# Routing of a mixture-of-experts stage: token rows stored without their shift, ranks by pairs, a gather straight from the table, four PSUM banks for the first expert

## The chip, the cores and the metric

One core of a Trainium2 chip runs the whole program. The metric is device time in microseconds (us) of one execution, the median of the runs shown. The engines are TensorE (PE; its weight loads stand apart as PEld), VectorE (DVE), ScalarE (ACT), GpSimd (POOL, which issues the DMAs with indices) and SyncE (SP, which issues the weight loads). Each runs its own instructions in order; they wait for each other by semaphores.

## What is computed

One layer of token mixers over 512 tokens of width 2048, then a grouped top-2 mixture-of-experts feed-forward, then an RMS norm. The change lies between the two: in the routing, and in how an expert's token block is read.

```python
hl2 = rmsnorm(xl, norm2_w[i]) * (1 + mod_l[4]) + mod_l[3]        # mod_l[3] is "m3" in the kernel

def moe_ffn(h, w_router, router_bias, w1, w3, w2):               # T = 512, 16 experts in 4 groups
    scores = sigmoid(h @ w_router)
    sel = scores + router_bias
    grp = sel.reshape(T, 4, 4)
    g_idx = argmax(top_k(grp, 2)[0].sum(-1))                     # best group by its two best experts
    _, loc = top_k(in_grp, 2)                                    # two experts of that group
    gate = gate / sum(gate)
    # tokens are sorted by expert into blocks of 128; a block is one expert's
    yblk = (silu(xblk @ w1[e]) * (xblk @ w3[e])) @ w2[e]
    # the two outputs of a token are weighted by gate and added
```

## The kernel before, in words

All matrices are fp32. A product is made of three matmuls on a high and a low part in fp32r: ACT writes the high part as a cast, DVE subtracts it from the source to give the low part.

**Rows.** DVE builds `x2` (tokens after the mixers) and `h2 = x2 * n2`, both `[128, 4, 2048]`: four tiles of 128 tokens. `normed(t)` (L1797) turns tile t into `h2 * inv_rms + m3` with `m3_row`, a row of 2048 values repeated on all partitions, and POOL stores it to `h2_d` in DRAM (L2160; the profile calls the tensor `h_rows`, and drops digits from all names, so that `m3_row` is `m_row`).

**Routing.** It is one chain on DVE. After the logits (L1802, L1805) ACT takes the sigmoid (L1281). `rank` (L1816 to L1825) gives each of four values its place by comparing with each other one: a memset, and six comparisons each followed by an addition. It runs over 64 values (experts) and again over 16 (groups). From the ranks come `chosen_r`, the gates, and from PE a count (L910, L912); after that `normed(2)` and `normed(3)`, then the places of the tokens, `in_block`, the one-hot `slot_1` (L1886), and from PE (L918) the table `table_i` (L1898): for each block the 128 token numbers. `step` waits for the instruction just issued. PE fills the time with `keep_busy` matmuls (L904), whose results nobody reads.

**Gather.** POOL copies a column of the table to `idx_now` (L2168), waits for the copy, and issues an indirect DMA (L2171) that brings 128 rows of `h2_d` into `xe`. It waits before the first for the table and for the landing of all four row tiles (`y_out`).

**Experts.** For each of 16 experts: `turn_x(b, part)`, part 0 to 3, four PE transposes each (L952) of `xe` into PSUM bank `6 + part % 2`; `x_hi` on ACT (L1292) casts the bank to `xe_hi`; `x_lo` on DVE (L1903) makes `xe_lo` from bank and `xe_hi`. There are two banks, so `turn_x` of a part waits for `x_lo` two parts back (L949; the semaphore `xe_rdy` begins at 2). Then come 24 units of weights, 128x1024 each and 6 matmuls each: 16 for the two up matrices, 8 for the down matrix. SP loads two units per DMA into one of 6 slots `e_raw` (L551), ACT casts (L1288, `e_hi`), DVE subtracts (L1809, `e_lo`).

The first expert stands outside a loop: its four `turn_x`, `x_ready(0)`, 16 up units, then the four `turn_x(1, ...)`. The loop `Fori(1, E)` runs 15 times over 24 units q: 16 up units of expert e, 8 down units of expert e - 1, and after units 17 to 20 a `turn_x` of expert e + 1:

```python
for q in range(24):                       # DVE, L1941 and after; PE and ACT alike
    e_lo_unit(e * 24 + (n - 8), n + 4)    # n = q + 5: five units ahead of PE
    if q == 3: act_lo(e - 1)
    if q == 9: silu(e)
    if q == 17: gate_up(e, ...)
    if 18 <= q <= 21: x_lo(e + 1, q - 18)
```

**Loads around the routing.** SP issues e_raw loads 0 to 3 early; load 4 waits for all four `normed`, load 5 for the landing of the stored rows, load 6 for the gather.

Of the kernel before, what the change touches and what calls it, by code (L numbers as in the profile page):

```python
# [32 lines left out]
P = 128  # L33
# [16 lines left out]
E = 16  # L50
# [80 lines left out]
def build(nc, x, c, ctx_tokens, c_ctx, w_ada, b_ada, norm1_w, norm2_w, w_in, w_pool_group, pool_scale,  # L131
# [22 lines left out]
    with stack:  # L154
# [119 lines left out]
        x2T = Room(nc, base, 90, 98).new("x2T", [P, 4, SEQ], F32)  # L274
        m3_row = Room(nc, base, 154, 162).new("m3_row", [P, D], F32)
        rt_room = Room(nc, base, 194, 198)
# [18 lines left out]
        gate_w = keep.new("gate_w", [P, 2, NTOK], F32)  # L295
        table_i = keep.new("table_i", [P, NBLK + 1], I32)
        idx_now = keep.new("idx_now", [P, 1], I32)
        route_i = keep.new("route_i", [P, 8], I32)
# [6 lines left out]
        block_tok = tb.new("block_tok", [P, 2 * NTOK, NBLK], F32)  # L305
        block_tok_r = tb.new("block_tok_r", [P, 2 * NTOK, NBLK + 1], F32R)
        slot_1 = tb.new("slot_1", [P, 2 * NTOK, P], F32R)

# [45 lines left out]
        def halves(pair, first, width, half):  # L354

            return bass.AP(pair.tensor, first, [[2 * SEQ, P], [2 * half, width // (2 * half)], [SEQ + half, 2],
                                                [1, half]])

        def bank(b, n=512):
            return ps[:, b, 0:n]  # L360
# [96 lines left out]
        def _(sp):  # L457
# [99 lines left out]
            for n in range(8):  # L557
                if n == 2:
                    sp.wait_ge(x2_rdy, 20)
                if n == 3:  # L560
                    sp.wait_ge(part_mm, 4)
                if n == 4:
                    sp.wait_ge(h2_rdy, NTOK)
                if n == 5:
                    sp.wait_ge(y_out, 16 * NTOK)
                if n == 6:
                    sp.wait_ge(xe_in, 16)
                load_e(n, n % EP, piece(0, n))
# [21 lines left out]
        def _(pe):  # L590
# [311 lines left out]
            def keep_busy(n):  # L902
                for _ in range(n):
                    mm(bank(UB), upper_r[:], m_hi[:, 8, :], start=True, stop=True)  # L904

            keep_busy(28)
            pe.wait_ge(sel_rdy, 1)
# [14 lines left out]
            pe.wait_ge(table_rdy, 1)  # L922
            keep_busy(24)

# [19 lines left out]
            def turn_x(b, part):  # L944

                if part == 0:
                    pe.wait_ge(xe_in, b * 16 + 16)

                pe.wait_ge(xe_rdy, b * 4 + (part + 1))  # L949
                pe.wait_ge(actT_rdy, b + 1)  # L950
                for j in range(4):
                    last = pe.transpose(ps[:, 6 + part % 2, j * P:(j + 1) * P],  # L952
                                        xe[:].rearrange("t (p k) -> t k p", k=KT)[:, 4 * part + j, :], ident[:])
                last.then_inc(xe_T, 1)
# [8 lines left out]
            def x_ready(b):  # L963
                pe.wait_ge(xe_rdy, b * 4 + 6)

            for part in range(4):
                turn_x(0, part)
            x_ready(0)
            for q in range(16):
                up_unit(q, q % EH, q % 8, q // 8)  # L970
            for part in range(4):
# [47 lines left out]
        def _(act_e):  # L1019
# [260 lines left out]
            act_e.wait_ge(lg_step, LG_RDY)  # L1280
            activate(rt[:, 0, :], rt[:, 3, :], ACT.Sigmoid).then_inc(lg_step, 1)  # L1281


# [27 lines left out]
            for q in range(AHEAD):  # L1311
                e_hi_unit(q, q, 16 * (q // 2 // EP + 1))
            act_e.wait_ge(table_rdy, 1)
            for part in range(4):
                x_hi(0, part)
# [60 lines left out]
        def _(dve):  # L1376
# [403 lines left out]
            modulated(3, 0)  # L1780
            dve.wait_ge(units_done, 2 + S_W + 32)
            own.did(dve.tensor_copy(ones_r[:], ones[:]))
            own.did(dve.memset(SM(15), 0.0))
# [27 lines left out]

            def rank(value, out, scratch, width):

                v, o, s = (a.rearrange("p (g a) -> p g a", a=4) for a in (value, out, scratch))
                n = width // 4
                step(dve.memset(out, 0.0))  # L1816
                for b in range(4):
                    if b < 3:
                        r = s[:, :, b + 1:4]
                        step(tt(r, v[:, :, b:b + 1].to_broadcast([P, n, 3 - b]), v[:, :, b + 1:4], ALU.is_ge))  # L1820
                        step(tt(o[:, :, b + 1:4], o[:, :, b + 1:4], r, ALU.add))
                    if b > 0:
                        r = s[:, :, 0:b]
                        step(tt(r, v[:, :, b:b + 1].to_broadcast([P, n, b]), v[:, :, 0:b], ALU.is_gt))
                        step(tt(o[:, :, 0:b], o[:, :, 0:b], r, ALU.add))  # L1825

            normed(1)
            dve.wait_ge(lg_step, LG_SCORE)
            step(tt(R3(1), R3(0), bias_row[:].unsqueeze(1).to_broadcast([P, NTOK, E]), ALU.add))
            rank(R(1), R(2), R(3), NTOK * E)  # L1830
# [3 lines left out]
            rank(SM(0), SM(1), SM(2), NTOK * GROUPS)  # L1834
            win_g = SM(3)
# [13 lines left out]

            normed(2)  # L1850
            normed(3)
            dve.wait_ge(pos_mm, 1)
# [141 lines left out]
        def _(pool):  # L1994
# [140 lines left out]
            pool.dma_start(bias_row[:], router_bias.partition_broadcast(P)).then_inc(rows_in, 16)  # L2135
            pool.dma_start(m3_row[:], mod_d[0, D:2 * D].partition_broadcast(P)).then_inc(rows_in, 16)

# [131 lines left out]
```

## Time and profile before

| what | value |
|---|---|
| median of 3 runs (lowest, highest) | 2394.51 us (2394.19, 2394.67) |
| the profiled execution, its own time | 2394.57 us |
| its span in the profile | 2393.0 us |
| PE busy | 2202.5 us, 92% of the span |
| DVE busy | 1545.9 us, 65% |
| ACT busy | 988.3 us, 41% |
| POOL busy | 524.9 us, 22% |
| mean granted TensorE clock | 0.96 of full speed |

Times inside the profile count from the start of the span. A row of the timeline gives start, length, engine, line, operation, output<-input, how many instructions it merges, and in brackets the idle time ahead of it with what ended it. A row of stretches gives each engine's busy time with its instructions, then the granted clock, the DMA share and GB/s.

### The profile page before, as it was taken

Reading aid. Unit: us, or ns where it says so; the run is one execution under the profiler, and the core shown is the slowest. Engines: PE = TensorE matmul, PEld = TensorE weight load, DVE = VectorE, ACT = ScalarE, POOL = GpSimd, SP = SyncE. Lnnn points to the kernel's source line nnn. Section 1 sums busy time; section 2 is a strip of 40 time slices with the busy share of each in tenths; the row PEclk is TensorE's granted clock in tenths of the full one; section 3 lists DMA queues with packets and bytes.
Section 4 is the critical chain, followed back from the end, with each engine's and each line's share of the span. In section 5 each row is a group of like instructions: output and inputs, shape, how many; then the busy total and the mean of one; then the engine's idle time right before and its main releaser. Section 6 shows DMA issues by size and latency. Waiting matters only on the chain. (4 is left out here: it accounts for less than half of the span.)

```text
span 2393.0 us, 33739 instructions
## 1 busy us (share of the span) xinstructions
PE 2202.5 (92%) x10804; PEld 1804.3 (75%) x10804; DVE 1545.9 (65%) x1913; ACT 988.3 (41%) x1199; POOL 524.9 (22%) x669
## 2 busy tenths in 40 slices
PE   4589999999999999899999999899889999999970
PEld 2089888888888887577778777678678888888860
DVE  2177645665666555566566655543679999999966
ACT  3044422333233323322222222232258888888862
POOL 0035524534453445011111111100000011011001
PEclk9789999999999999899999999899899999999995
DMA  8945462222232223466777665834489999999955
GB/s 355 385 118 164 145 208 82 87 74 81 81 88 75 78 82 92 163 219 220 220 235 232 211 220 183 266 119 150 159 327 399 416 415 420 420 417 417 420 241 210
DMA packets 326492, 532.14 MB, mean 222 GB/s; under 512 B 12160, under 2 KB 258448, under 8 KB 294448
## 3 DMA queue, kind: packets, MB, share of 16 engines
q1 hardware_dynamic: 292832, 392.92, 46.1%
q0 software_dynamic: 33616, 138.65, 16.1%
q8 instruction: 26, 0.43, 0.1%
q14 instruction: 18, 0.15, 0.0%
HBM read 494.79 MB, written 36.73 MB: 222 GB/s over the span
## 5 line engine op out<-in xcount | busy, mean ns | idle before, releaser
L1422 DVE TENSOR_TENSOR w_lo<-raw,w_hi 128x1024 fp32r<-128x1024 f32 x272 | 351.3, 1292 | 411.0 <-ACT w_hi L1049 410.7
L1049 ACT CAST w_hi<-raw 128x1024 fp32r<-128x1024 f32 x272 | 284.9, 1047 | 660.0 <-PE ps L648 322.2
L646 PE MATMUL ps<-hl_hi,w_hi 128*128 128x512 f32 x1280 | 509.1, 398 | 0.5 <-DVE s_ctx L1495 0.5
L648 PE MATMUL ps<-hl_hi,w_lo 128*128 128x512 f32 x1280 | 499.1, 390 | 0.0
L647 PE MATMUL ps<-hl_lo,w_hi 128*128 128x512 f32 x1280 | 499.0, 390 | 0.0
L1809 DVE TENSOR_TENSOR e_lo<-e_raw,e_hi 128x1024 fp32r<-128x1024 f32 x384 | 455.6, 1220 | 50.1 <-ACT e_hi L1288 37.1
L1288 ACT CAST e_hi<-e_raw 128x1024 fp32r<-128x1024 f32 x384 | 399.4, 1059 | 86.9 <-PE ps L932 86.8
L648 PEld LDWEIGHTS ps<-hl_hi,w_lo 128*128 128x128 f32 x1280 | 240.7, 188 | 50.9
L646 PEld LDWEIGHTS ps<-hl_hi,w_hi 128*128 128x128 f32 x1280 | 241.0, 188 | 49.8 <-issue 1.7
L647 PEld LDWEIGHTS ps<-hl_lo,w_hi 128*128 128x128 f32 x1280 | 241.1, 188 | 49.2 <-issue 1.7
L930 PE MATMUL ps<-e_hi,xe_hi 128*128 128x512 f32 x512 | 202.1, 395 | 4.3 <-DVE e_lo L1809 2.9
L932 PE MATMUL ps<-e_hi,xe_lo 128*128 128x512 f32 x512 | 200.6, 392 | 0.0
L931 PE MATMUL ps<-e_lo,xe_hi 128*128 128x512 f32 x512 | 200.4, 391 | 0.0
L1652 DVE SCALAR_TENSOR_TENSOR ada_acc<-ada,silu_c,ada_acc 128x512 f32<-128x512 f32 x240 | 180.2, 751 | 7.0 <-DMA ada<-in_w_ada 0.2
L646 PE MATMUL ps<-hc_hi,w_hi 128*128 128x256 f32 x384 | 113.2, 295 | 14.1 <-DVE w_lo L1422 7.6
L2179 POOL DMA_DIRECT2D block_outputs<-y_sb x32 | 17.4, 544 | 487.6 <-ACT y_sb L1308 481.5
L930 PEld LDWEIGHTS ps<-e_hi,xe_hi 128*128 128x128 f32 x512 | 97.1, 190 | 24.3 <-DVE e_lo L1809 3.1
L932 PEld LDWEIGHTS ps<-e_hi,xe_lo 128*128 128x128 f32 x512 | 96.8, 189 | 20.5
L871 PE MATMUL ps<-w_hi,m_hi 128*128 128x512 f32 x256 | 102.1, 399 | 10.9 <-DVE m_lo L1698 10.9
L931 PEld LDWEIGHTS ps<-e_lo,xe_hi 128*128 128x128 f32 x512 | 96.9, 189 | 19.8
L648 PE MATMUL ps<-hc_hi,w_lo 128*128 128x256 f32 x384 | 110.8, 289 | 0.0
L647 PE MATMUL ps<-hc_lo,w_hi 128*128 128x256 f32 x384 | 110.8, 289 | 0.0
(341 smaller groups left out, 3550.7 us busy)
## 6 DMA issues: line engine op xcount, KB each, us to landing
e_raw<-in_w_e SPq DMA_DIRECT2D x192, 1024.0 KB, 9.8
raw<-in_w_in SPq DMA_DIRECT2D x208, 512.0 KB, 3.7
ada<-in_w_ada POOLq DMA_DIRECT2D x64, 1024.0 KB, 6.1
ada_ring<-in_w_ada SPq DMA_DIRECT2D x16, 2048.0 KB, 16.6
raw<-in_w_out SPq DMA_DIRECT2D x32, 512.0 KB, 3.8
block_outputs<-y_sb POOLq DMA_DIRECT2D x32, 512.0 KB, 6.6
raw<-in_w_branch_pool SPq DMA_DIRECT2D x16, 512.0 KB, 3.9
raw<-in_w_branch_hgrn SPq DMA_DIRECT2D x16, 512.0 KB, 3.9
```

The costliest lines, as they stand in the source:

```text
L646: mm(dst, hi, rhs_hi[:, k, :], start=(k == 0), stop=False)
L647: mm(dst, hi, rhs_lo[:, k, :], start=False, stop=False)
L648: last = mm(dst, lo, rhs_hi[:, k, :], start=False, stop=(k == KT - 1))
L871: mm(bank(t), a_hi, hi, start=(k == 0), stop=False)
L930: mm(bank(b), a_hi, hi, start=start, stop=False)
L931: mm(bank(b), a_hi, lo, start=False, stop=False)
L932: last = mm(bank(b), a_lo, hi, start=False, stop=stop)
L1049: act_e.copy(w_hi[:, hslot, :], raw[:, slot, :]).then_inc(hi_done, 1)
L1288: act_e.copy(e_hi[:, n % EH, :], e_raw[slot][:, n % 2, :]).then_inc(e_hi_done, 1)
L1422: tt(w_lo[:, hslot, :], raw[:, slot, :], w_hi[:, hslot, :].bitcast(F32), ALU.subtract).then_inc(split_done, 1)
L1652: ins = stt(out=acc[:], in0=w, scalar=cs[:, 0, k:k + 1], in1=acc[:], op0=ALU.mult, op1=ALU.add)
L1809: tt(e_lo[:, n % EH, :], e_raw[n // 2 % EP][:, n % 2, :], e_hi[:, n % EH, :].bitcast(F32), ALU.subtract).then_inc(e_split, 1)
```

## The change

Token rows are stored as `h2 * inv_rms`, without m3; m3 lies as a column `m3_col` (partition p holds features 16p to 16p + 15, as the transposed `xe` has them) and is added in `x_hi` and `x_lo`. Since the column differs from one of the 16 slices of 128 columns to the next, each 128x512 cast and each 128x512 subtraction become four instructions of 128x128. `normed(0)` and `(1)` stay on DVE as a multiplication by one column, `(2)` and `(3)` go to ACT. `rank` compares all 16 pairs of four in one instruction and takes six instructions in place of 13. The first two gathers read their index column from the table itself, and the loads of `m5_row` and `fn_row` stand behind the second gather. The first expert's four parts have four banks (6, 7, 2, 3), and its up units wait part by part. SP's load 4 no longer waits. `keep_busy` has 18 for 28 and, behind the table, 12 for 24.

```diff
-        m3_row = Room(nc, base, 154, 162).new("m3_row", [P, D], F32)
+        m3_col = keep.new("m3_col", [P, KT], F32)
...
+        def x_bank(b, part):
+            return (6, 7, 2, 3)[part] if isinstance(b, int) and b == 0 else 6 + part % 2
...
-                if n == 4:
-                    sp.wait_ge(h2_rdy, NTOK)
...
-            keep_busy(28)
+            keep_busy(18)
...
             pe.wait_ge(table_rdy, 1)
-            keep_busy(24)
+            keep_busy(12)
...
-                pe.wait_ge(xe_rdy, b * 4 + (part + 1))
-                pe.wait_ge(actT_rdy, b + 1)
+                if not (isinstance(b, int) and b == 0):
+                    pe.wait_ge(xe_rdy, b * 4 + (part + 1))
+                    pe.wait_ge(actT_rdy, b + 1)
...
             for part in range(4):
                 turn_x(0, part)
-            x_ready(0)
             for q in range(16):
+                if q < 8 and q % 2 == 0:
+                    pe.wait_ge(xe_rdy, q // 2 + 3)
                 up_unit(q, q % EH, q % 8, q // 8)
...
             activate(rt[:, 0, :], rt[:, 3, :], ACT.Sigmoid).then_inc(lg_step, 1)
+            act_e.wait_ge(x2m_rdy, 16)
+            act_e.wait_ge(h2_rdy, 2)
+            for t in range(2, NTOK):
+                activate(h2[:, t, :], h2[:, t, :], ACT.Copy, scale=stat2[:, 3, t:t + 1]).then_inc(h2_rdy, 1)
...
             def x_hi(b, part):
                 act_e.wait_ge(xe_T, b * 4 + (part + 1))
-                act_e.copy(xe_hi[:, 4 * part:4 * part + 4, :].rearrange("p k t -> p (k t)"), bank(6 + part % 2)
-                           ).then_inc(xe_hi_rdy, 1)
+                for j in range(4):
+                    k = 4 * part + j
+                    last = activate(xe_hi[:, k, :], ps[:, x_bank(b, part), j * BLK:(j + 1) * BLK], ACT.Identity,
+                                    bias=m3_col[:, k:k + 1])
+                last.then_inc(xe_hi_rdy, 1)
...
             def normed(t):
-                stt(out=h2[:, t, :], in0=h2[:, t, :], scalar=stat2[:, 3, t:t + 1], in1=m3_row[:],
-                    op0=ALU.mult, op1=ALU.add).then_inc(h2_rdy, 1)
+                ts(h2[:, t, :], h2[:, t, :], stat2[:, 3, t:t + 1], None, ALU.mult).then_inc(h2_rdy, 1)
 
             normed(0)
+            normed(1)
...
+                over, net = (pairs[:, i, 0:16 * n].rearrange("p (g a b) -> p g a b", a=4, b=4) for i in range(2))
+                step(tt(over, v.unsqueeze(3).to_broadcast([P, n, 4, 4]), v.unsqueeze(2).to_broadcast([P, n, 4, 4]),
+                        ALU.is_ge))
+                step(tt(over, over, earlier[:].unsqueeze(1).to_broadcast([P, n, 4, 4]), ALU.mult))
+                step(tt(net, over.rearrange("p g a b -> p g b a"), over, ALU.subtract))
+                step(dve.tensor_reduce(o, net, AX.X, ALU.add))
+                step(tt(o, o, iota[:, 0:4].unsqueeze(1).to_broadcast([P, n, 4]), ALU.subtract))
+                step(ts(out, out, 3.0, None, ALU.add))
...
-            normed(2)
-            normed(3)
             dve.wait_ge(pos_mm, 1)
...
             def x_lo(b, part):
                 dve.wait_ge(xe_hi_rdy, b * 4 + (part + 1))
-                tt(xe_lo[:, 4 * part:4 * part + 4, :].rearrange("p k t -> p (k t)"), bank(6 + part % 2),
-                   xe_hi[:, 4 * part:4 * part + 4, :].rearrange("p k t -> p (k t)").bitcast(F32), ALU.subtract
-                   ).then_inc(xe_rdy, 1)
+                for j in range(4):
+                    k = 4 * part + j
+                    last = stt(out=xe_lo[:, k, :], in0=ps[:, x_bank(b, part), j * BLK:(j + 1) * BLK],
+                               scalar=m3_col[:, k:k + 1], in1=xe_hi[:, k, :].bitcast(F32),
+                               op0=ALU.add, op1=ALU.subtract)
+                last.then_inc(xe_rdy, 1)
...
-            gather(0, 0)
+            gather_now(0)
+            pool.wait_ge(xe_in, 16)
+            pool.wait_ge(xe_T, 4)
+            gather_now(1)
             pool.dma_start(m5_row[:], mod_d[0, 3 * D:4 * D].partition_broadcast(P)).then_inc(rows_in, 16)
             pool.dma_start(fn_row[:], final_norm_w.partition_broadcast(P)).then_inc(rows_in, 16)
-            pool.wait_ge(xe_in, 16)
-            pool.wait_ge(xe_T, 4)
-            gather(1, 1)
```

How the instructions stand, in two places. First DVE, from the second tile's `normed` to the end of the rank over the 64 expert values, before:

```order
L1797 SCALAR_TENSOR_TENSOR h_133<-h_133,stat_156,m_row 128x2048
L1829 TENSOR_TENSOR rt<-rt,bias_row 128x64
L1816 MEMSET rt 128x64
L1820 TENSOR_TENSOR rt<-rt 128x16x3
L1821 TENSOR_TENSOR rt<-rt 128x16x3
L1820 TENSOR_TENSOR rt<-rt 128x16x2
L1821 TENSOR_TENSOR rt<-rt 128x16x2
L1824 TENSOR_TENSOR rt<-rt 128x16
L1825 TENSOR_TENSOR rt<-rt 128x16
```

and DVE of the change, from both `normed` to the end of that rank:

```order
L1813 TENSOR_SCALAR h_133<-h_133,stat_156 128x2048 x2
L1818 TENSOR_TENSOR rt<-ps,stat_156 128x64
L1821 TENSOR_TENSOR rt<-rt,m_logit 128x64
L1842 TENSOR_TENSOR rt<-rt,bias_row 128x64
L1833 TENSOR_TENSOR pairs<-rt 128x256
L1835 TENSOR_TENSOR pairs<-pairs,earlier 128x256
L1836 TENSOR_TENSOR pairs<-pairs 128x256
L1837 TENSOR_REDUCE rt<-pairs 128x64
L1838 TENSOR_TENSOR rt<-rt,iota 128x64
L1839 TENSOR_SCALAR rt<-rt 128x64
```

The second `normed` now stands ahead of the logits; the rank has four wide instructions and two short ones (before, four more pairs of short ones follow the rows shown).

Second DVE in the loop over the experts, around the first two `x_lo`, before:

```order
L1918 TENSOR_TENSOR act<-ps,act_u 128x512
L1808 REGISTER_ALU
L1809 TENSOR_TENSOR e_lo<-e_raw_164,e_hi 128x1024
L1902 ISA
L1903 TENSOR_TENSOR xe_lo<-ps,xe_hi 128x512
L1808 REGISTER_ALU
L1809 TENSOR_TENSOR e_lo<-e_raw_165,e_hi 128x1024
L1902 REGISTER_ALU
L1903 TENSOR_TENSOR xe_lo<-ps,xe_hi 128x512
```

and of the change:

```order
L1932 TENSOR_TENSOR act<-ps,act_u 128x512
L1824 REGISTER_ALU
L1825 TENSOR_TENSOR e_lo<-e_raw_166,e_hi 128x1024
L1913 ISA
L1916 SCALAR_TENSOR_TENSOR xe_lo<-ps,m_col,xe_hi 128x128 x4
L1824 REGISTER_ALU
L1825 TENSOR_TENSOR e_lo<-e_raw_167,e_hi 128x1024
L1913 REGISTER_ALU
L1916 SCALAR_TENSOR_TENSOR xe_lo<-ps,m_col,xe_hi 128x128 x4
```

Each `x_lo` is four instructions at the place where one stood; nothing changed places around it.

## Rows read from the trace of the kernel before

**Rows 1.** Stretches: time, PE, PEld, DVE, ACT, POOL busy, clock, DMA share, GB/s

```profile
1706.00:1714.00 8.00, 7.29 (x27) 5.42 (x28) 7.17 (x19) 5.75 (x8) 1.09 (x2) 0.60 1.01 394
...
1726.00:1733.30 7.30, 0.00 (x1) 0.00 (x0) 6.51 (x28) 0.00 (x0) 0.53 (x1) 0.65 1.00 303
...
1749.10:1752.20 3.10, 3.08 (x8) 2.46 (x9) 1.23 (x1) 0.24 (x2) 0.73 (x1) 0.53 1.03 433
...
1800.00:2300.00 500.00, 500.00 (x2340) 417.72 (x2339) 457.93 (x443) 421.02 (x485) 43.64 (x56) 1.00 1.01 416
```

**Rows 2.** Timeline of DVE in the routing

```profile
1712.36 0.22 DVE L1829 TENSOR_TENSOR rt<-rt,bias_row 128x64 f32<-128x64 f32 x1
1712.66 0.11 DVE L1816 MEMSET rt<- 128x64 f32 x1
...
1715.59 0.23 DVE L1832 SCALAR_TENSOR_TENSOR rt<-rt 128x64 f32<-128x64 f32 x1
...
1716.14 0.07 DVE L1816 MEMSET rt_small<- 128x16 f32 x1
...
1718.69 0.17 DVE L1836 TENSOR_SCALAR rt_small<-rt_small 128x16 f32<-128x16 f32 x1
...
1721.38 4.61 DVE L1797 SCALAR_TENSOR_TENSOR h<-h,stat,m_row 128x2048 f32<-128x2048 f32 x2
...
...
1729.93 0.36 DVE L1874 TENSOR_TENSOR in_block<-rt_small,rt 128x192 f32<-128x192 f32 x1
...
1735.68 0.17 DVE L1898 CAST table_i<-ps 128x23 int32<-128x23 f32 x1
```

**Rows 3.** Timeline of POOL and ACT: the first gather, the sigmoid

```profile
1736.09 0.95 POOL L2168 COPY idx_now<-table_i 128x1 int32<-128x1 int32 x1 [9.27 <-DVE table_i L1898]
1737.94 1.09 POOL L2171 DMA_INDIRECT xe<-h_rows,idx_now  x1 [0.90 <-POOLq L85]
...
1710.21 0.26 ACT L1281 ACTIVATE rt<-rt 128x64 f32<-128x64 f32 x1 [1.20 <-DVE rt L1805]
```

**Rows 4.** Timeline of PE: the first expert's start and the second's

```profile
1744.23 1.17 PE L952 MATMUL ps<-ident,xe 128*128 128x128 f32 x8
...
1749.12 0.80 PE L930 MATMUL ps<-e_hi,xe_hi 128*128 128x512 f32 x1 [1.40 <-DVE xe_lo L1903]
...
1772.59 1.17 PE L952 MATMUL ps<-ident,xe 128*128 128x128 f32 x8
...
1778.95 0.50 PE L930 MATMUL ps<-e_hi,xe_hi 128*128 128x512 f32 x1 [2.88 <-DVE e_lo L1809]
```

**Rows 5.** Groups by form: busy us, mean ns of one

```profile
L1542 DVE SCALAR_TENSOR_TENSOR S_f<-S_f,T_f,ps 128x128 f32<-128x128 f32 x24 | 8.4, 348 | 0.9
...
L123 DVE TENSOR_TENSOR c_kg<-c_kg,c_f 128x128 f32<-128x128 f32 x8 | 2.3, 285 | 0.0
...
L1412 DVE TENSOR_SCALAR x_tok<-x_tok,stat 128x2048 f32<-128x2048 f32 x6 | 7.4, 1283 | 0.1
...
L1204 ACT ACTIVATE poolT<-ps,vecT 128x512 f32<-128x512 f32 x8 | 5.5, 688 | 12.7 <-PE ps L806 12.7
```

**Rows 6.** Timeline of one turn of the expert loop: DVE, PEld, PE

```profile
1983.94 0.68 DVE L1903 TENSOR_TENSOR xe_lo<-ps,xe_hi 128x512 fp32r<-128x512 f32 x1
1984.54 1.21 DVE L1809 TENSOR_TENSOR e_lo<-e_raw,e_hi 128x1024 fp32r<-128x1024 f32 x1
1985.67 0.68 DVE L1903 TENSOR_TENSOR xe_lo<-ps,xe_hi 128x512 fp32r<-128x512 f32 x1
...
1989.14 0.68 DVE L1903 TENSOR_TENSOR xe_lo<-ps,xe_hi 128x512 fp32r<-128x512 f32 x1
...
1984.67 0.57 PEld L952 LDWEIGHTS ps<-ident,xe 128*128 128x128 f32 x4
...
1986.44 0.66 PEld L952 LDWEIGHTS ps<-ident,xe 128*128 128x128 f32 x4
...
1991.01 0.39 PE L932 MATMUL ps<-e_hi,actT_lo 128*128 128x512 f32 x1
```

More of the change, by code:

```diff
@@ L306, in build @@
         block_tok_r = tb.new("block_tok_r", [P, 2 * NTOK, NBLK + 1], F32R)
+        pairs = tb.new("pairs", [P, 2, 16 * NTOK * GROUPS], F32)
+        earlier = tb.new("earlier", [P, 4, 4], F32)
         slot_1 = tb.new("slot_1", [P, 2 * NTOK, P], F32R)
@@ L947, in turn_x @@
                     pe.wait_ge(xe_in, b * 16 + 16)
-                pe.wait_ge(xe_rdy, b * 4 + (part + 1))
-                pe.wait_ge(actT_rdy, b + 1)
+                if not (isinstance(b, int) and b == 0):
+                    pe.wait_ge(xe_rdy, b * 4 + (part + 1))
+                    pe.wait_ge(actT_rdy, b + 1)
                 for j in range(4):
-                    last = pe.transpose(ps[:, 6 + part % 2, j * P:(j + 1) * P],
+                    last = pe.transpose(ps[:, x_bank(b, part), j * P:(j + 1) * P],
                                         xe[:].rearrange("t (p k) -> t k p", k=KT)[:, 4 * part + j, :], ident[:])
@@ L1313, in _ @@
             act_e.wait_ge(table_rdy, 1)
+            act_e.wait_ge(rows_in, 5 * 16)
             for part in range(4):
@@ L1781, in _ @@
             dve.wait_ge(units_done, 2 + S_W + 32)
+            own.did(tt(earlier[:], iota[:, 0:4].unsqueeze(1).to_broadcast([P, 4, 4]),
+                       iota[:, 0:4].unsqueeze(2).to_broadcast([P, 4, 4]), ALU.is_gt))
             own.did(dve.tensor_copy(ones_r[:], ones[:]))
@@ L1810, in e_lo_unit, with rank @@
                    ).then_inc(e_split, 1)
-            def rank(value, out, scratch, width):
-                v, o, s = (a.rearrange("p (g a) -> p g a", a=4) for a in (value, out, scratch))
+            def rank(value, out, width):
                 n = width // 4
[L1816 to L1827, printed above, removed]
+                v, o = (t.rearrange("p (g a) -> p g a", a=4) for t in (value, out))
+                over, net = (pairs[:, i, 0:16 * n].rearrange("p (g a b) -> p g a b", a=4, b=4) for i in range(2))
[6 more added lines that the diff above has]
+                step(ts(out, out, 3.0, None, ALU.add))
             dve.wait_ge(lg_step, LG_SCORE)
             step(tt(R3(1), R3(0), bias_row[:].unsqueeze(1).to_broadcast([P, NTOK, E]), ALU.add))
-            rank(R(1), R(2), R(3), NTOK * E)
+            rank(R(1), R(2), NTOK * E)
             step(stt(out=R(4), in0=R(2), scalar=2.0, in1=R(1), op0=ALU.is_lt, op1=ALU.mult))
             step(dve.tensor_reduce(SM(0), R4(4), AX.X, ALU.add))
-            rank(SM(0), SM(1), SM(2), NTOK * GROUPS)
+            rank(SM(0), SM(1), NTOK * GROUPS)
             win_g = SM(3)
@@ L2135, in _ @@
             pool.dma_start(bias_row[:], router_bias.partition_broadcast(P)).then_inc(rows_in, 16)
-            pool.dma_start(m3_row[:], mod_d[0, D:2 * D].partition_broadcast(P)).then_inc(rows_in, 16)
+            pool.dma_start(m3_col[:], mod_d[0, D:2 * D].rearrange("(p k) -> p k", k=KT)).then_inc(rows_in, 16)
             def load_block(cb):
@@ L2179, in store, with gather_now @@
                     pool.dma_start(y_d[ds(b * BLK, BLK), cols], y_sb[:, cols]).then_inc(y_out, 16)
-            gather(0, 0)
+            def gather_now(column):
+                pool.indirect_dma_start(out=xe[:], out_offset=None, in_=h2_d,
+                                        in_offset=bass.IndirectOffsetOnAxis(ap=table_i[:, column:column + 1], axis=0)
+                                        ).then_inc(xe_in, 16)
+            gather_now(0)
+            pool.wait_ge(xe_in, 16)
+            pool.wait_ge(xe_T, 4)
+            gather_now(1)
             pool.dma_start(m5_row[:], mod_d[0, 3 * D:4 * D].partition_broadcast(P)).then_inc(rows_in, 16)
             pool.dma_start(fn_row[:], final_norm_w.partition_broadcast(P)).then_inc(rows_in, 16)
-            pool.wait_ge(xe_in, 16)
-            pool.wait_ge(xe_T, 4)
-            gather(1, 1)
             with pool.Fori(1, E) as e:
```

## The prediction

> **What bounds the kernel now.** I read the stretches first, then the timelines of the routing, then one turn of the expert loop. From 1800 to 2300 us PE is busy 500.00 of 500 at full clock, DVE 457.93, ACT 421.02 [rows 1]: the experts cost what PE's matmuls cost. Before them PE does nothing useful: between 1726 and 1733.3 not one matmul starts, and DVE goes from one short routing step to the next [rows 1, 2]. So the routing is bounded by DVE's chain, then by the gather, then by how fast `xe` is turned and split. What is saved there moves everything behind it; what makes PE wait in the loop counts 15 times. The sum is made against the profiled execution, 2394.57 us, 0.06 above the median of 2394.51. A measurement here can tell from no change about 0.2%, 4.8 us.
>
> **The routing chain on DVE.** *Logits.* Two `normed` by one column cost 1.28 each, as L1412, 1.20 from start to start [rows 5]; with them ahead of the logits the sigmoid starts as before, at 1710.2, and ends at 1710.47 [rows 3]. L1829 follows at about 1710.5 in place of 1712.36 [rows 2]: -1.85. *First rank:* 1712.66 to 1715.59, 2.93 [rows 2]. A step of 192 elements takes 0.39 from start to start (0.36 and a gap), one of 64 0.26 (0.22 and the gap) [rows 2], so 256 take 0.46. Four of these and two of 64 are 2.35: -0.6. *Second rank:* 1716.14 to 1718.69, 2.55; four steps of 64 and two of 16 (0.2 each) are 1.45: -1.1. *Two `normed` of 4.61, 4.53 less the overlap* [rows 2], go to ACT, which is free: -4.5. The count from PE they hid was asked for at `chosen_r`, some 1.8 us of gate steps ahead of its use, which cover it still, and 18 `keep_busy` end about when it is wanted. `earlier` lies beside a wait: nothing. The table is then written at 1727.6 instead of 1735.68: **-8.05**.
>
> **The rows in DRAM.** They must have landed by then. SP's load 4 no longer waits, so five loads and four stores of 1.05 MB are asked for from 1702 on; at 394 GB/s [rows 1] they end at about 1726. This hides behind the table by 1 to 2 us only.
>
> **The gather.** The copy and the gap behind it (1736.09 to 1737.94) [rows 3] go: -1.85. The gather took from 1737.94 to PE's first transpose at 1744.23 [rows 3, 4], 6.3, with SP's load 5 and two row loads of 1 MB beside it; without these two I take 5.6, and 5 to 6.3 as bounds: -0.7. PE would turn `xe` at 1733.6. Its `keep_busy` might last to 1733.8, since part of it runs at the low clock after the idle stretch: I count **-10.4** to the first transpose.
>
> **Turning and splitting, first expert.** Before: 1744.23 to 1749.12, 4.89 [rows 4]. An `x_lo` instruction of the change reads PSUM, a column and an SBUF tensor, as L1542 does: 348 ns; without the column (L123) it is 285 [rows 5]. DVE's instructions start 0.08 before the last one ends (0.68 long, 0.60 apart) [rows 6], so the pitch is **0.265**, and a part takes 1.06 in place of 0.60. For ACT: L1204, 512 columns from PSUM with a column, is 688 ns [rows 5]; 384 columns less at 0.84 give 0.365, pitch 0.27. By these the first matmul comes 0.8 (transposes) + 1.2 (ACT) + 1.15 (DVE) + 0.1 = 3.25 after the first transpose, since it needs only part 0: -1.65. The later parts take 1.1 each, PE needs one each 2.7. The first matmuls ran at 0.53 of the clock until 1752.2 [rows 1], 7 of them 0.2 slower; with PE nearly without a pause before them I count on the high clock: -1.45. Together **-13.5** at the first expert.
>
> The Trainium skill (ScalarE: Activation LUTs, What ACT_TABLE_LOAD costs) says that each column operand adds about 93 ns and gives 280 ns plus 0.833 ns an element, 387 here, 294 back to back. By that ACT would take 0.1 more per part, and the sum would be about 0.4 higher than the one below.
>
> **Second expert's turn.** Two banks again, and now the parts are longer. Before 1772.59 to 1778.95, 6.36 [rows 4]. The chain T0, `x_hi` 0, `x_lo` 0, T2, `x_hi` 2, `x_hi` 3, `e_hi`, `e_lo` becomes 3.2 to T2, 4.0 and 5.1 to the two `x_hi`, 6.2 to `e_hi`, 7.4 to `e_lo`, 8.6 to the matmul: +2.3, and some more matmuls at the low clock, +0.5. **-10.7** remains at the loop.
>
> **The loop.** Here is the term that decides. `turn_x` of part 2 waits for `x_lo` 0. That ends at 1984.62, and the weight load of the transpose starts at 1984.67 [rows 6]: it is held already, by as much as costs nothing. The one of part 3 starts at 1986.44 with `x_lo` 1 ending at 1986.35 [rows 6]. Now `x_lo` 0 ends 0.46 later. `x_lo` 1 starts 0.46 later (one DVE queue: `e_lo` between them is pushed back) and ends 0.92 later, at 1987.27; PE's load follows at 1987.32, 0.88 late, of which some 0.1 is hidden by its overlap. PE is thus 0.78 late in each turn, at part 3. Nothing takes this back: PE is the bound. ACT has 0.3 of idle per unit there and its `x_hi` 0 still ends 0.4 before DVE asks for it. The low parts of the weights are five units ahead, so DVE's 1.84 more per turn don't reach PE that way. 15 turns: **+11.7**. The bounds are 0.20 as pitch (the column costs nothing, 285 less 83 ns), 0.25 a turn, and 0.348 (no overlap), below.
>
> The Trainium skill (VectorE: DVE Perf Modes, The TRN2 errata) advises against small tiles and gives 120 cycles plus one per element for PSUM to SBUF, at 0.96 GHz: 258 ns for 128 and 658 for 512. By these a part would grow by 0.37, a turn by about 0.6, the loop by 9, and the sum would be 2 below the kernel before. The row of 348 ns speaks for the higher cost.
>
> **Sum.** -8.05 - 1.85 - 0.7 + 0.2 (`keep_busy`) = -10.4; - 1.65 - 1.45 + 2.3 + 0.5 = -10.7; + 11.7 = **+1.0**: 2395.6.
>
> **The rivals.**
> *The column is free* (faster). DVE's pitch is 0.20, a turn loses 0.25, the loop 3.7: 2394.6 - 10.7 + 3.7 = 2387.6. For it: TENSOR_TENSOR at 128 elements has this pitch. Against it: L1542 is 63 ns longer [rows 5]. 0.12.
> *PE has room in the loop* (faster): the loads of the transposes are prefetched and the wait costs nothing, so 2383.9 stays. Against it: the load at 1984.67 starts 0.05 behind its `x_lo` [rows 6]. 0.05.
> *The end of the turn decides* (slower). The loop's next `x_ready` waits for the last `x_lo`. That ends at 1989.82, and PE's first load of the next turn is due at 1991.01 [rows 6]; at a pitch of 0.265 the four parts end 1.84 later, the load is 0.7 late, 0.6 without the overlap, just under the 0.78 above. Each ns of pitch adds 7 ns at part 3 but 15 there, so from 0.29 on this wait decides, and with 0.348 the last ends 3.1 later: 1.85 a turn, 27.7 in all, 2411. For it: nothing in the trace shows these forms in a row of four. Against it: all of DVE's instructions overlap by 0.08. 0.13 for anything from 0.29 up.
> *The rows land late.* Nine transfers at the 303 GB/s of the stretch with the last stores [rows 1] end at 1733, not 1726, and the gather starts 5 us later: 2400.6. It decides below about 365 GB/s. Against it: that stretch begins with only two stores and a load in flight. 0.06.
> *Forecast* 0.64.
>
> **How the numbers follow.** Likeliest 2395.6; its own range 2391 to 2400, from pitch 0.25 to 0.285 (a ns of it is 0.1 us over the loop), gather 5 to 6.3, and the clock terms, 1.5 either way. The range for 8 in 10 goes from 2389 to 2402, short of both ends of the rivals. Faster by over 0.2% (below 2389.7): the two faster rivals, 0.16. Slower (above 2399.3): the end of the turn, late rows and a tail of the forecast, 0.19. Within: 0.65.
>
> **What would show it.** In the changed profile: table at 1727.6 and gather at 1728.0; first transposes at 1733.5 to 1734; 3.2 to the first matmul; `x_lo` instructions of about 0.35, 0.265 apart; PE waits named "PE ps L952 <- DVE xe_lo" twice a turn, together about 0.8; a turn of 35.9 us in place of 35.1; PE below 500 of 500 in the loop. I am wrong if a turn still takes 35.1, or more than 36.2, or if the gather waits for the stores.

## The result and the profile after

| | before | after |
|---|---|---|
| median of 17 runs, us | 2394.72 | 2398.67 |
| lowest to highest, us | 2392.75 to 2396.80 | 2396.65 to 2401.38 |
| profiled execution: its time, its span, us | 2394.57, 2393.0 | 2398.67, 2397.0 |
| ratio, 95% interval | | 1.0016 [1.0008, 1.0023] |

The change makes the kernel slower by 3.95 us, 0.16%. That is less than the 0.2% named above, but with 17 runs a side the interval leaves out no change. The forecast was 2395.6 us, 3.1 below, in a range that holds the result.

The routing came out much as forecast. DVE's timeline after the change, which answers to [rows 2] (start, duration, engine, line, operation):

```profile
1707.48 2.48 DVE L1813 TENSOR_SCALAR h<-h,stat 128x2048 f32<-128x2048 f32 x2
1710.70 0.22 DVE L1842 TENSOR_TENSOR rt<-rt,bias_row 128x64 f32<-128x64 f32 x1 [0.32 <-ACT rt L1287]
1710.96 0.42 DVE L1833 TENSOR_TENSOR pairs<-rt 128x256 f32<-128x256 f32 x1
...
1711.87 0.62 DVE L1836 TENSOR_TENSOR pairs<-pairs 128x256 f32<-128x256 f32 x1
...
1713.46 0.23 DVE L1845 SCALAR_TENSOR_TENSOR rt<-rt 128x64 f32<-128x64 f32 x1
...
1715.53 0.17 DVE L1849 TENSOR_SCALAR rt_small<-rt_small 128x16 f32<-128x16 f32 x1
...
1728.01 0.17 DVE L1909 CAST table_i<-ps 128x23 int32<-128x23 f32 x1
```

The table is written 7.67 us earlier (1728.01 in place of 1735.68). The timelines of SP, POOL and PE between the table and the first expert answer to [rows 3, 4]:

```profile
1728.07 0.33 SPq L557 DMA_DIRECT2D e_raw<-in_w_e  x1
1729.07 1.15 POOL L2196 DMA_INDIRECT xe<-h_rows,table_i  x1 [13.55 <-DVE table_i L1909]
```

```profile
1726.57 4.82 PE L908 MATMUL ps<-m_hi,upper_r 128*128 128x512 f32 x20
1736.84 3.68 PE L957 MATMUL ps<-ident,xe 128*128 128x128 f32 x16 [5.45 <-DMA xe<-h_rows,table_i]
1740.44 0.79 PE L934 MATMUL ps<-e_hi,xe_hi 128*128 128x512 f32 x1
...
1763.12 1.17 PE L957 MATMUL ps<-ident,xe 128*128 128x128 f32 x8
1766.29 0.71 PE L957 MATMUL ps<-ident,xe 128*128 128x128 f32 x4 [2.00 <-DVE xe_lo L1916]
...
1771.57 0.79 PE L934 MATMUL ps<-e_hi,xe_hi 128*128 128x512 f32 x1 [3.52 <-DVE e_lo L1825]
```

Three things are to be seen. SP issues a weight load at 1728.07, a full microsecond ahead of the gather. PE sits idle for 5.45 us before the first transposes. And the first transposes are 7.39 us earlier than before, not the 10.4 of the forecast. Then the loop. First the stretch 1800 to 2300 us (columns as in [rows 1]), then what PEld waits for there (total, times, longest), then DVE's timeline of one turn:

```profile
1800.00:2300.00 500.00, 497.00 (x2290) 407.24 (x2289) 470.46 (x601) 439.50 (x643) 45.54 (x56) 1.00 1.00 407
```

```profile
PEld ps L957 <- DVE xe_lo L1916: 15.0, 28, 0.7
```

```profile
1980.74 1.12 DVE L1916 SCALAR_TENSOR_TENSOR xe_lo<-ps,m_col,xe_hi 128x128 fp32r<-128x128 f32 x4
1981.79 1.21 DVE L1825 TENSOR_TENSOR e_lo<-e_raw,e_hi 128x1024 fp32r<-128x1024 f32 x1
1982.92 1.12 DVE L1916 SCALAR_TENSOR_TENSOR xe_lo<-ps,m_col,xe_hi 128x128 fp32r<-128x128 f32 x4
```

The new wait stands in the rows of PEld, the weight loads of the transposes, and hardly in those of PE. It comes twice a turn, 28 times in these 500 us. From the first transpose of one turn to that of the next it is 35.80 us (35.09 before); this is called the turn below. The positions of the first transposes give the whole account, profile against profile:

| first transpose of | before | after | difference |
|---|---|---|---|
| first expert | 1744.23 | 1736.84 | -7.39 |
| second expert | 1772.59 | 1763.12 | -9.47 |
| third expert | 1805.69 | 1798.74 | -6.95 |
| seventeenth block (14 turns on) | 2296.97 | 2300.16 | +3.19 |
| last instruction of the program | 2392.97 | 2397.02 | +4.05 |

### The profile page after: what moved, and what is told of

It is laid out like the page before. It is cut to its first block, busy times and chain, and to the rows that moved or that the text cites. A ratio compares the mean times of both kernels' runs of the same rounds, so it can differ in the third digit from the quotient of the medians.

```text
span 2397.0 us, 34086 instructions
## 1 busy us (share of the span) xinstructions
PE 2201.1 (92%) x10782; PEld 1796.5 (75%) x10782; DVE 1564.8 (65%) x2102; ACT 1024.3 (43%) x1405; POOL 525.4 (22%) x667
## 4 chain that ended last, share of the span: by engine, by line
PE 75%; DVE 5%; issue 3%; DMA 3%; ACT 1%; POOL 1%; POOLq 0%; SPq 0%; DVEq 0%; ACTq 0%
PE ps L650 12%; PE ps L652 12%; PE ps L651 12%; PE ps L934 6%; PE ps L936 6%; PE ps L935 6%; PE ps L875 3%; PE ps L877 2%; PE ps L876 2%; PE ps L821 2%; PE ps L823 2%; PE ps L822 2%; PE ps L710 2%; DVE xe_lo L1916 1%; DVE e_lo L1825 1%
```

## Experiments

Twelve kernels were run, each beside the kernel before on the same chip. The medians of the kernel before lay between 2394.82 and 2396.01 us there, so that medians of different groups of runs compare to about 1 us. Four of the kernels take the loop apart first, since it decides the sign.

**Whole pieces in the loop.** The first expert keeps its pieces; `x_lo` is changed likewise.

```diff
             def x_hi(b, part):
                 act_e.wait_ge(xe_T, b * 4 + (part + 1))
+                if not (isinstance(b, int) and b == 0):
+                    act_e.copy(xe_hi[:, 4 * part:4 * part + 4, :].rearrange("p k t -> p (k t)"), bank(6 + part % 2)
+                               ).then_inc(xe_hi_rdy, 1)
+                    return
```

> The changed kernel with x_hi and x_lo of every expert but the first put back to one 128x512 instruction a part (m3 is left out of those experts' tokens). Theory A, the small pieces are what lengthens the loop: the turn goes from 35.80 back to 35.09 us, 14 turns give 9.9 us and the ends beside them about 1, so 2388 us against 2398.7 (ratio to the kernel before 0.997). Rival B, the loop is longer because of something in the routing part (weights that arrive later, another order of loads): the turn stays at 35.8 and the time at 2398 to 2399. The second expert's turn, 33.10 us before and 35.62 after, falls under A to about 33.5; under the rival that the earlier start lacks weights it stays above 35.

Measured: 2383.62 us, ratio 0.9953 [0.9939, 0.9966]; the turn is 35.09 again. Rival B falls: the loop is longer by its pieces alone. The time is 4 us below what was expected. In this profile the gather took 6.60 us to the first transpose and not 7.77, and the first expert's transposes ran at the high clock (first product 3.19 us behind the first transpose, against 3.60), which is worth 1 us more. The second expert's turn is 34.39: less than the 35.62 of the change, but not the 33.5 that was expected.

**Pieces in the kernel before.** The same two operations in four pieces each, with a column of zeros in place of m3, all else as before.

> The kernel before, with x_hi and x_lo in four 128x128 pieces a part and a column of zeros as the operand; the result is unchanged. Theory A: the turn goes from 35.09 to 35.8 us, 14 turns cost 9.9 us; with the first expert's parts (each about 0.5 longer, in one chain) and the second expert's turn about 3 more, 2407 us against 2394.7 (ratio 1.005). Rival B: the turn stays at 35.09 and the time within 2 us of 2394.7.

Measured: 2414.02 us, 1.0080 [1.0067, 1.0094]. The turn is 35.80 us, so the size of the loop term is confirmed from the other side. The sum was missed by 7 us. With two banks and `x_ready` for all parts, the pieces cost 3.1 us at the first expert (31.44 in place of 28.36 to the second's transposes), 3.2 at the second, and three turns of the loop were longer than 35.80 by 0.1 to 1.1. At the first expert PE waits there 2.0 and 0.3 us for a bank and 2.4 us for the last `x_lo`; in the change it waits for neither. Four banks and the part-wise waits are thus what keeps the pieces cheap at the first expert.

**DVE's pieces or ACT's.** Two kernels, each with one of the two operations put back to a whole from the second expert on.

> The changed kernel with x_hi of every expert but the first as one 128x512 copy, and x_lo still in four pieces (x_lo then takes all of m3). Theory A1, the pieces on DVE are the cost: the turn is 35.5 to 35.8 us, 2395 to 2398.7 us. Rival A2, the pieces on ACT are: the turn is 35.1 to 35.2, 2388 to 2391 us. If both count, 35.4 to 35.5.

> The changed kernel with x_lo of every expert but the first as one 128x512 subtraction, and x_hi still in four pieces (m3 cancels, so it is left out of those experts' tokens). Theory A1, DVE's pieces are the cost: the turn is 35.1 to 35.3 us, 2388 to 2391 us. Rival A2, ACT's are: 35.6 to 35.8 us, 2396 to 2398.7 us.

Measured: with DVE's pieces 2396.64 us, 1.0011 [1.0002, 1.0020], turn 35.80; with ACT's 2386.63 us, 0.9966 [0.9954, 0.9978], turn 35.09. What PEld waits for in the kernel with DVE's pieces alone:

```profile
PEld ps L957 <- DVE xe_lo L1920: 14.8, 28, 0.6
```

With ACT's alone there is no such row. So the whole 0.71 us a turn is DVE's, and ACT's pieces cost the loop nothing, though they add 24 us of busy time to ACT in 500 (421.75 in the kernel with whole pieces, 446.11 here).

**The next transposes set wider apart.** If the wait comes from DVE being asked for two parts within two weight units, it should go once a second unit lies between the last parts. `X_AT` is (17, 18, 20, 22).

```diff
-                    if 17 <= q <= 20:
-                        turn_x(e + 1, q - 17)
+                    if q in X_AT:
+                        turn_x(e + 1, X_AT.index(q))
...
-                x_ready(e)
+                pe.wait_ge(xe_rdy, e * 4 + 5)
...
+                    if q == 6:
+                        pe.wait_ge(xe_rdy, e * 4 + 6)
```

> The changed kernel with the third and fourth part of the next expert's transposes moved from the units 19 and 20 of a turn to 20 and 22 (x_hi and x_lo follow by one unit, the fourth part is awaited only at unit 6 of the next turn). Theory A1, PE waits since x_lo's parts come closer on DVE than DVE gets them done: with a second weight unit between them the wait goes, the turn is 35.09 to 35.2 us and the time 2388 to 2390 us, with m3 added per feature in full. Rival H, DVE as a whole is now full over a turn (470 us busy of 500): the turn stays above 35.5 and the time within 2395 to 2399 us.

Measured: 2391.28 us, 0.9983 [0.9974, 0.9992], with m3 added in full. The turn is 35.13. The stretch 1800 to 2300, and DVE's timeline at the same place as above:

```profile
1800.00:2300.00 500.00, 500.00 (x2340) 417.87 (x2338) 480.32 (x620) 446.11 (x662) 45.70 (x56) 1.00 1.00 412
```

```profile
1976.74 1.12 DVE L1918 SCALAR_TENSOR_TENSOR xe_lo<-ps,m_col,xe_hi 128x128 fp32r<-128x128 f32 x4
...
1978.91 1.12 DVE L1918 SCALAR_TENSOR_TENSOR xe_lo<-ps,m_col,xe_hi 128x128 fp32r<-128x128 f32 x4
1979.95 2.35 DVE L1827 TENSOR_TENSOR e_lo<-e_raw,e_hi 128x1024 fp32r<-128x1024 f32 x2
1982.22 1.12 DVE L1918 SCALAR_TENSOR_TENSOR xe_lo<-ps,m_col,xe_hi 128x128 fp32r<-128x128 f32 x4
```

DVE does the same work per turn, in a turn that is shorter by 0.67 us, and PE is busy 500.00 of 500. DVE was never full: it was asked for the wrong thing at the wrong moment. (The edit also lets the last part be awaited later, at unit 6. That is not what helped: in the change nothing in the loop waits at `x_ready`, since the only waits for `x_lo` are those of the transposes.) One execution of this kernel out of 11 took 6120.27 us, the others 2389.57 to 2392.49. Nothing recorded says why, and in 10 executions of the two kernels below that are built on it this did not recur.

**The load ahead of the gather.** In the change, SP's sixth load waits for the stored rows alone. It now waits for the first gather.

```diff
                 if n == 5:
-                    sp.wait_ge(y_out, 16 * NTOK)
-                if n == 6:
                     sp.wait_ge(xe_in, 16)
```

> The changed kernel with the sixth weight load of the first expert held until the first gather has landed (before it waited for the stored rows alone, was issued 1.0 us ahead of the gather, and its 1.05 MB moved from 1729 to 1732 while the gather's first packets went at 1731.8). Theory C, that load stands ahead of the gather: the gather lands about 2.5 us earlier (1734.3 in place of 1736.8), the first transposes come as much earlier, and the time falls by 2 to 2.5 us to about 2396.4. Rival D, the gather takes its 7 us whatever moves beside it: the first transposes stay at 1736.8 and the time at 2398.7. Rival E, the load is missed later: the transposes come earlier, but the first expert's up units wait for weights, and the time is the same or up to 2 us longer.

Measured: 2396.19 us, 1.0006 [0.9997, 1.0015]. The gather and the first transposes:

```profile
1729.14 1.15 POOL L2194 DMA_INDIRECT xe<-h_rows,table_i  x1 [13.56 <-DVE table_i L1907]
```

```profile
1735.39 2.07 PE L955 MATMUL ps<-ident,xe 128*128 128x128 f32 x16 [2.32 <-DMA xe<-h_rows,table_i]
```

From the gather's issue to the first transpose it is 6.25 us, in place of 7.77. The packets in the trace show how. In the change those of the load run from 1729.0 to 1732.2 and those of the gather begin at 1731.9, 2.85 us after its issue; here they begin 1.85 us after it.

What the load costs hangs on its lead over the gather. In the six profiles in which it is issued 0.75 to 1.15 us ahead, the gather takes 7.2 to 8.1 us; in two (whole pieces, and the weights in hand first) it is 1.6 and 1.7 us ahead, and the gather takes 6.6 and 6.5. In the kernel before it is 2.6 us ahead, its packets are through before the gather's begin, and the gather takes 6.29. With the load held back, three profiles give 6.25, 6.24 and 6.54. So C is right in kind, but worth 1.5 us here and not 2.5, and the gather alone does not get below 6.2 (D).

The median fell by 2.5 us (by 3.8, with each kernel set against the kernel before beside it), but the two intervals overlap. The clock stayed high at the transposes in this profile, which may be the rest; it did so without this edit too, and that the edit brings it is not shown.

**More dummy matmuls.** `keep_busy(12)` behind the table becomes `keep_busy(32)`.

> The changed kernel with 32 dummy matmuls in place of 12 after the table, so that they last until about 1735.9 and not 1731.4, just short of the first transposes at 1736.84. Theory F, the idle 5.45 us cost the clock (0.66 granted from 1737 to 1744): the transposes last 277 ns and not 417, the first up units run at 2.4 GHz, and the time falls by 1.5 to 2.5 us to 2396 to 2397. Rival G: the first expert waits for DVE's and ACT's pieces, not for PE, so no more than 0.7 us is won.

Measured: 2399.07 us, 1.0017 [1.0008, 1.0026]: nothing is won. Two stretches of the change, then the same two of this kernel (the last three columns are the clock, DMA and GB/s):

```profile
1736.00:1740.00 4.00, 3.16 (x15) 3.16 (x16) 0.74 (x3) 1.92 (x8) 0.00 (x0) 0.50 0.55 184
...
1765.00:1800.00 35.00, 29.86 (x128) 24.54 (x129) 32.73 (x42) 28.70 (x40) 1.18 (x2) 0.90 0.85 322
```

```profile
1736.00:1740.00 4.00, 2.82 (x20) 2.17 (x18) 0.88 (x4) 2.05 (x9) 0.05 (x1) 1.00 0.49 156
...
1765.00:1800.00 35.00, 30.56 (x127) 24.95 (x128) 32.18 (x40) 27.89 (x36) 1.19 (x2) 0.85 0.86 323
```

The first half of F holds: PE stays at 2.4 GHz through the transposes, and the second expert's come after 25.31 us in place of 26.28. But the turn that follows is 36.55 in place of 35.62. PE pauses there in both kernels for 2.0, 0.3 and 3.5 us, and the granted clock behind that pause is 0.85 over the 35 us, not 0.90. What the dummies saved in front was lost one turn on. That this had to be so is not shown: with the load held back the clock was high at the first transposes too (second expert after 25.32 us), and the turn behind was 35.05, the clock of the same stretch 0.90. The low stretch behind the pause lasted 6.8 us there and in the change, and 10.2 us in three profiles (this one, the next one and that of the spread transposes). What decides between the two was not found.

**Both edits together**, with 22 dummies:

> Both of the two edits before: the sixth load behind the gather, and 22 dummy matmuls after the table (to about 1733.6). Under C and F together the first transposes stand at 1734.3 at 277 ns each, and the time is 2398.7 less 4 to 5, about 2394. Under D or E with F: 2396 to 2398, with a stretch of low clock after the dummies end.

Measured: 2397.22 us, 1.0007 [0.9998, 1.0016]. The two do not add: the gather takes 6.24 us here too, but the second expert's turn is again 36.55.

**The weights in hand first.** Both the change and the runs above spend up to 5.8 us of PE's time at the second expert. The weights for it landed 12 us and more before they were split: DVE and ACT had queued `x_lo` and `x_hi` ahead of them.

```diff
             for q in range(16):
                 n = q + AHEAD
-                if n < 16:
+                if n < 16 + AHEAD:
                     e_lo_unit(n, n)
...
-            for n in range(AHEAD):
-                e_lo_unit(16 + n, 16 + n)
...
-            return (6, 7, 2, 3)[part] if isinstance(b, int) and b == 0 else 6 + part % 2
+            return (6, 7, 2, 3)[part] if isinstance(b, int) and b < 2 else 6 + part % 2
```

ACT's `e_hi_unit` is changed like DVE's `e_lo_unit`. All this is put on top of the spread transposes; the waits for `x_lo`'s parts stand at the units 0, 2 and 6 of a turn.

> The kernel with the spread parts (2391.28 us), and in it: the five weight units that follow the first expert's sixteen are split ahead of the second expert's x_hi and x_lo on ACT and DVE, and the second expert's transposes use four banks as the first's do. In the changed kernel's trace PE waits 2.3 us for xe_lo and 3.5 us for e_lo there, though these weights had landed 12 us before. Theory I: both waits go, the stretch from the second expert's first transpose to its first product falls from 8.4 to about 4 us, and the time by 4 to 5 us to 2386.5 to 2387.5. Rival J: the time is given back within the second turn, since loads follow the splits and come no earlier: not under 2389.5.

Measured: 2384.32 us, 0.9954 [0.9941, 0.9968], the fastest kernel here with m3 in full. PE's timeline at the second expert, and its clock from 1766 to 1778:

```profile
1760.45 2.08 PE L959 MATMUL ps<-ident,xe 128*128 128x128 f32 x16
1763.70 0.49 PE L934 MATMUL ps<-e_hi,xe_hi 128*128 128x512 f32 x1 [1.18 <-DVE xe_lo L1920]
```

```profile
1766.00:1778.00 12.00, 12.00 (x57) 9.98 (x56) 11.73 (x14) 10.28 (x12) 0.00 (x0) 1.00 1.01 423
```

```profile
1766.00:1778.00 12.00, 8.33 (x27) 6.57 (x28) 10.74 (x17) 10.25 (x17) 1.19 (x2) 0.59 0.65 229
```

The second of the two stretches is that of the kernel with the spread transposes alone. From transpose to product it is 3.25 us, in place of 8.45 in the change and 8.85 in the kernel with the spread transposes alone, and the low clock behind it is gone. The second expert's turn is 28.38 us in place of that kernel's 36.38: 5.6 of the 8.0 us lie ahead of the product, 2.4 behind it, where the clock no longer falls. J falls. The gain is larger than expected: 7.0 us between the medians, 5.8 with each kernel set against the kernel before beside it. The order of the weights and the four banks were changed together, and which of them brings how much was not measured.

> The run before this one together with the sixth load held behind the first gather. Alone that edit took 2.5 us from the changed kernel (2396.19 us). If the two add up: 2384 to 2385. If the earlier start finds weights missing: the same as the run before this one, within 1 us.

Measured: 2386.35 us, 0.9960 [0.9946, 0.9973]. That is 2.0 us above the run before it, where 1 was allowed for; the two intervals overlap, so neither a gain nor a loss is shown. The second expert's turn is 31.06. What ACT waits for from 1740 to 1800 us:

```profile
ACT e_hi L1302 <- DMA e_raw<-in_w_e: 2.6, 2, 1.8
```

In the run before there is no such row: with the pauses gone, the held load is missed. (The first transposes ran mostly at the low clock in this profile, too.)

> The kernel before, with only the order of the weight units around the second expert changed as in the best run: the five units after the first sixteen are split ahead of its x_hi and x_lo. In the trace of before PE waits 2.9 us there for e_lo and twice 1.0 for xe_lo (two banks, which stay). Theory K, this gain belongs to the kernel before as well and not to the change: the 2.9 us go, and 2391 to 2392.5 us follow, so that of the 10.5 us by which the best run (2384.32) is below before some 3 are not the change's. Rival: before has no weights at hand there, and the time stays within 1 us of 2394.8.

Measured: 2393.83 us, 0.9997 [0.9988, 1.0006]: no change. The wait of 2.9 us for `e_lo` did go, but behind it stood one of 1.5 us for `xe_lo`, since the two banks and `x_ready` are still there; 6.36 us became 5.03. The low clock behind the pause was longer too (6.8 us in place of 3.4), as in the run with more dummies. So theory K falls: in the kernel before, order alone wins nothing. That the gain needs what the change brings along, four banks and waits by part, is argued from this pair of runs; four banks without the new order were not run.

**m3 added by POOL.** Another way to keep whole pieces: POOL adds the row to `xe` once the gather has landed.

> The changed kernel, but from the second expert on POOL adds m3 to the gathered tokens (two 128x1024 additions in xe once the gather has landed, the row in two 4 KB tiles), and x_hi and x_lo are one 128x512 instruction a part as before the change; the first expert keeps its pieces. POOL's 128x512 f32 additions lasted 1.4 to 1.8 us in the trace, so the two halves take 6 to 7.5 us of some 25 us that a gather has until its tokens are due. Theory: POOL is idle 90% of the loop, so the turn is 35.09 and the time that of the run with whole pieces, 2384 us, with m3 added in full. Rival: POOL's additions slow DVE's or the loads beside them (DVE's e_lo then longer than 1221 ns on average), and the turn is 35.3 or more, 2387 us and up.

Measured: 2457.50 us, 1.0262 [1.0247, 1.0276], 62.7 us above the kernel before. DVE and POOL in one turn:

```profile
1866.24 7.92 DVE L1834 TENSOR_TENSOR e_lo<-e_raw,e_hi 128x1024 fp32r<-128x1024 f32 x3
1867.12 5.96 POOL L2229 TENSOR_TENSOR xe<-xe,m_row 128x1024 f32<-128x1024 f32 x2 [11.31 <-DMA xe<-h_rows,idx_now]
```

```profile
L1834 DVE TENSOR_TENSOR e_lo<-e_raw,e_hi 128x1024 fp32r<-128x1024 f32 x303 | 407.0, 1394 | 46.5 <-ACT e_hi L1303 46.0
...
L962 PE MATMUL ps<-ident,xe 128*128 128x128 f32 x204 | 38.0, 317 | 37.6 <-DVE xe_lo L1924 37.6
```

Three `e_lo` take 7.92 us; three at 1.13 from start to start would take 3.5. Here the two that begin while an addition runs last 3.43 us each and the others 1.21 to 1.23. The additions last 2.61 and 3.39 us, and each of the two long subtractions ends 1.1 us after an addition has ended. DVE loses 4.4 us in this turn, and the turns grow to between 36.8 and 41.0 us. The Trainium skill (SBUF — State Buffer, SBUF: two separate sides) calls the port pair of the two engines an exclusive lock, which a DVE operation with two SBUF inputs takes too, against a GpSimd operation that reads SBUF; the other of the two is blocked for the whole instruction. The trace agrees, by the 3.43 us in place of 1.22. A DVE that is busy 457.93 us of 500 [rows 1] has nothing to lend.

## Why the prediction came out as it did

The steps, in its own order:

| step | forecast | measured |
|---|---|---|
| table | -8.05 | -7.67 |
| gather issued, from the table's write | 0.4 | 1.06 |
| gather's issue to first transpose | 5.6 | 7.77 |
| first transpose, in all | -10.4 | -7.39 |
| to the first product | 3.25 | 3.60 |
| first expert to second, in all | -3.1 | -2.08 |
| second expert's turn | +2.8 | +2.52 |
| a turn of the loop | +0.78 | +0.71 |
| rest of the loop, in all | +11.7 | +10.84 |
| behind the loop | 0 | +0.16 |
| sum | +1.0 | +4.05 |

The misses are +3.0 at the first transpose, +1.0 from there to the second expert, -0.3 in its turn, -0.9 in the loop and +0.2 behind it, 3.05 in all. The range of 2391 to 2400 held the result because it was wide enough for the gather's miss, and the loop's shortfall gave back a part of it.

**The table.** The two instructions of `normed` cost the 4.5 that was counted, the second rank 1.55 in place of 1.45, the first 2.50 in place of 2.35, as the subtraction that reads `pairs` across (0.62 us) is longer than its neighbours (0.42). The sigmoid began 0.20 later (1710.41), and the gaps around the ranks were 0.07 shorter. The stage as a whole begins anywhere between 1705.9 and 1709.5 over the profiles of this case (1707.3 in the change), so that positions of two profiles compare no better than that unless their starts agree, as these two do to 0.3.

**The gather: the step that failed.** Of the forecast's steps this one missed by most: 2.8 us, where the whole sum missed by 3.05. "Without these two I take 5.6" counted 0.7 for the two row loads that no longer run beside the gather. They were worth nothing: 6.29 us with them before, 6.25 with neither them nor the weight load in the way. So 0.65 too little was taken for the gather by itself. The larger part is what else the change lets go at that moment. SP's sixth load waits for the stored rows. The prediction had them landed at 1726, and with them that load well ahead; they landed at 1728.0, about as the table was written. So the load was issued at 1728.07, 1.0 us ahead of the gather at 1729.07 and not 2.6 as before, and its megabyte went first: 1.5 us (7.77 against 6.25). The rest, 0.65, is the time between the table and the issue: the prediction took the 0.4 that POOL had needed for its copy, and this instruction needed 1.06.

**The clock.** "With PE nearly without a pause before them I count on the high clock" hung on the gather: the late gather made a pause of 5.45 us, and the 16 transposes ran at 417 ns and 1.2 GHz (granted clock 0.50 from 1736 to 1740 us). Where the clock stayed high, first product and second expert stood just where they were forecast: 3.19 us, and -3.05 in place of -3.1. In the runs with more dummies the time did not fall for it: there the second expert's turn took back what was won. With the load held back it did not, and why was not found.

**The loop: right.** `x_lo` lasts 345 ns and four of them 1.12 us from first to last end, a pitch of 0.26 (forecast 0.348 and 0.265). The mechanism, PE held at a transpose by `x_lo` two parts back, was shown by the runs that take it apart: it goes when DVE's piece is whole, stays when ACT's is, appears in the kernel before with the pieces, and goes when a unit is set between. The prediction put the lateness all at part 3; the weight loads wait 0.56 us at part 2 and 0.50 at part 3, and of these 1.06 us 0.71 reaches the turn (the forecast of 0.78 is right to 0.07). The name it gave, "PE ps L952", was not quite right: the wait stands at PEld. Nor was "PE below 500 of 500" a good sign: the kernel with whole pieces shows 497.35 in the stretch where the change shows 497.00, though its turn is 35.09 and nothing waits there.

**The rivals.** The column is not free (345 ns against 285). PE has no room in the loop. The end of the turn does not decide at a pitch of 0.26. The rows landed late by 2 us and not by 7; their harm was done by the load they release, which no rival had. The estimate of 258 ns for 128 elements from PSUM by the Trainium skill (VectorE: DVE Perf Modes, The TRN2 errata), weighed above and turned down for the row of 348, is close to the pitch of 260 ns measured here but not to the duration of 345; for 512 elements it gives 658 ns where the pitch is 600 and the duration 680 [rows 6]. The loop's 10.8 us lie between the 9 that followed from it and the 11.7 taken.

## What to carry to other kernels

Work that is moved from a part that runs once into a loop that runs 15 times has to be priced at its place in a turn: here 0.46 us more per part on an engine with 40 us of idle time in 500 cost PE 0.71 us a turn, and setting two parts one unit further apart gave nearly all of it back. When a wait is removed or comes earlier, list every transfer that the same event releases, since one of them may now stand ahead of the transfer that matters. A pause of PE can cost twice, itself and the clock behind it (here 5.6 and 2.4 us), so pauses are better removed than filled: with the first one filled the time stayed as it was (2399.07 against 2398.67 us), removing the second won 6 to 7 us.

## What the runs showed of the hardware

- A gather of 1.05 MB by 128 indices takes 6.2 to 6.5 us from its issue to the transposes that wait for it even with no weight load ahead of it. With a load of 1.05 MB issued 0.75 to 1.15 us before, it takes 7.2 to 8.1; with the same load 1.6 us or more before, 6.2 to 6.6.
- Four 128x128 instructions with a column operand keep a start-to-start distance of 0.26 us on DVE and 0.25 on ACT, though one lasts 345 and 397 ns: for work in a row the distance is the price, not the duration.
- An addition on POOL and a subtraction on DVE, both with two SBUF inputs, exclude each other: DVE's 1.22 us became 3.43.
- Of two profiles of the same routing code, one had the low clock at the first transposes and the other had not (first product after 3.60 or 3.19 us), which alone moves the time by 1 us. It went with PE's pause ahead of them. Over the eleven profiles of the change and its variants, the transposes ran at 277 ns behind pauses of up to 3.3 us (six profiles) and mostly or all at 417 ns behind 4.2 to 5.7 us (four); behind 3.5 us the clock fell among them. The pause hung on the dummy matmuls in turn: with a granted clock of 0.50 from 1726 to 1732.5 us (whole pieces) they lasted until 1734.67 and left 1.09 us, with 1.00 (the change) they ended at 1731.39 and left 5.45.
